# Spreading of a product-key expert layer: three chunks of the expert table rounded whole in the route, none in the first two steps, the next group rounded within the steps, and the last load moved into the experts' stage

## The chip, the cores and the metric

The kernel is one program on one NeuronCore of a Trainium2 chip. The metric is the device time of one execution in microseconds. Three runs of the kernel before gave 3746.18, 3740.43 and 3745.97 us, a median of 3745.97.

## The reference, cut to what matters

A decoder trunk of two layers over 512 tokens of 1024 channels, all in float32. Each layer is a token mixer with a layer norm and then a product-key expert layer (PEER) with a layer norm. The change lies in the expert layer:

```python
q = jnp.einsum('td,dn->tn', xt, wq).reshape(T, PEER_HEADS, 2, PEER_HALF)
s1 = jnp.einsum('thd,hkd->thk', q[:, :, 0], keys[0]); s2 = ...
v1, i1 = lax.top_k(s1, 16);  v2, i2 = lax.top_k(s2, 16)
cand = v1[..., :, None] + v2[..., None, :]           # 256 candidates a head
top_s, pos = lax.top_k(cand, 16)                     # of 128 x 128 experts
gate = jax.nn.softmax(top_s, axis=-1)
hidden = jax.nn.gelu(jnp.einsum('td,thkd->thk', xb, u_tab[eb]))
y = jnp.einsum('thk,thkd->td', gb * hidden, v_tab[eb])
```

## The kernel before, in words

The first 128 tokens ("far") take their experts' rows by gathers, with VectorE. For the other 384 tokens the kernel computes all 16384 experts densely: hidden = gelu(U x) by chunks of 128 experts, times a matrix of gates that is zero where an expert isn't chosen, times V. The table u comes in 32 groups of EC = 4 chunks, chunk = 128 experts x 1024 channels. A float32 product is made of two rounded parts: ScalarE copies a chunk of u (`ur`, raw) to its high part (`uh`), another engine subtracts to get the low part (`ul`), and TensorE multiplies three times (`matmul_split`, L97 to L99), 8 x 3 = 24 matmuls a chunk of 384 columns.

There are three stages, each an `nc.Block()` of its own with one program for each engine (sync = SP, gpsimd = POOL, tensor = PE, scalar = ACT, vector = DVE); no engine enters the next block before all have left the last one.

The route (`route_stage`, L1356 on) finds the experts of every token on VectorE, tile by tile of 128 tokens, while the other engines make the hidden values of 12 groups ahead. GpSimd makes all the low parts there (`ahead.low`, L1264). At its end come the first chunks of the next stage, by `high_for_next`, `low_for_next` (L1287) and `multiply_for_next`: chunk 0 is rounded and multiplied there, its low part by GpSimd; chunk 1 (SPLIT_AHEAD = 2) is rounded there only, its low part by VectorE after the last of its routing. That routing ends with six copy_predicated (L1599), a sum, a reciprocal and a product (L1605 to L1608); after it TensorE transposes rows, columns and gates (`turn`, L1443), and ScalarE keeps them (`keep_pairs`, L1489 to L1496).

Spreading (`spread_stage`) writes the gates, one 128 x 128 block a token, as products of one-hot matrices: 24 steps of 16 tokens. In step n VectorE makes one-hot rows (`find`, L1694, which waits until TensorE has left step n - 2, since `one_hot` and `hot_col` have two buffers) and three weighted copies (`weigh`, L1702); ScalarE makes four more rows (`one_hot_rows`, L1771 and L1774), TensorE runs four groups g of 12 matmuls (L1751), ScalarE copies each group's bank to `stage` (L1785), and SP stores two steps at a time (L1820). Beside this the stage makes the hidden values of 6 more groups, 24 chunks: a load of two chunks by SP (L1230, L897 for the next stage's), high part on ScalarE (L1259, L1282), low part on VectorE (L1264, L1287), matmuls after group g = 1, and a gelu. Before, `units_of` gives step n the second half of chunk n + 1 and the first half of chunk n + 2; `high_at` has ScalarE round chunk n + 3 in step n, `low_at` VectorE chunk n + 2. Chunks 24 and 25 are the first two of the experts' stage. Their fellows 26 and 27 are rounded after the last step, and SP issues the second half of the next group's u (`load_second(sp, 1)`) when those low parts are there. The experts' stage (`experts_stage`) begins with chunks 2 and 3 of its first group on TensorE (`hidden(0, MADE_FIRST)`).

Of the kernel before, what the change touches and what calls it, by code (L numbers as in the profile page):

```python
# [16 lines left out]
P = 128  # L17
# [3 lines left out]
KT = D_MODEL // P  # L21
# [17 lines left out]
EC = 4  # L39
# [5 lines left out]
NTB = TD // TB  # L45
AHEAD_ROUTE = 12
AHEAD_SPREAD = 6
SPLIT_AHEAD = 2
MADE_FIRST = 2
NG_AHEAD = AHEAD_ROUTE + AHEAD_SPREAD  # L50
NG_FULL = NG - NG_AHEAD
# [8 lines left out]
STEP = 16  # L60
# [54 lines left out]
def build_program(nc, a):  # L115

    with ExitStack() as whole:
# [21 lines left out]
        sem = Signals()  # L139
# [15 lines left out]
        xh = sb(whole, "xT_high", [P, KT, SEQ], F32R)  # L155
# [697 lines left out]
        for layer in range(DEPTH):  # L853
            with ExitStack() as upper:
# [76 lines left out]
                def closing_norm(ctx):  # L931
                    return Norm(ctx, "cl", carried[0], None, *carried[1:])

                experts_stage(nc, a, layer, sb, peer, bank, xh, xl, u, far, storing, sem, closing_norm, first_block, project_sems())
        kept.close()


# [422 lines left out]
def route_stage(nc, a, layer, sb, sem, bank, qT, keys, x, u, load_next, ident, iota_row, rowT, listed, gateT, gate_part,  # L1360
# [6 lines left out]
    with ExitStack() as ctx:  # L1367
# [39 lines left out]
        with nc.Block() as block:  # L1407
# [7 lines left out]
            @block.gpsimd  # L1415
            def _(pool):
                pool.sem_inc(ahead.u_low, 4)
                for chunk in range(EC * AHEAD_ROUTE):
                    ahead.low(pool, chunk // EC, chunk % EC)
                    if chunk == PER_TILE + 2:  # L1420
                        for m in range(RING):
                            far.gather(pool, m)
                ahead.low_for_next(pool, 0)

            @block.tensor
            def _(pe):
# [98 lines left out]
            def _(dve):  # L1525
                V = nc.vector
                link = make_link(dve, chain)
                for t in range(NT):
# [79 lines left out]
                    link(V.tensor_tensor(weights, gate[:], total[:].unsqueeze(2).to_broadcast([P, H, K]), ALU.mult))  # L1608
                    if t:
                        V.engine_nop().then_inc(routed, 1)  # L1610
                dve.wait_ge(ahead.next_low, 1)
                ahead.low_for_next(nc.vector, 1)


def spread_stage(nc, a, layer, sb, sem, bank, x, u, load_next, load_second, iota_row, rowT, listed, gateT, gate_part):
# [4 lines left out]
    with ExitStack() as ctx:  # L1620
# [23 lines left out]
        CHUNKS = EC * AHEAD_SPREAD  # L1644
        assert CHUNKS == STEPS

        def units_of(n):

            return [(n + 1, slice(KT // 2, KT))] * (n > 0) + [(n + 2, slice(0, KT // 2))]

        made = {c: max(c - 1, 0) for c in range(CHUNKS)}
        high_at = {c - 3: c for c in range(2, CHUNKS + 2)}
        low_at = {c - 2: c for c in range(2, CHUNKS + 2)}
        load_at, store_at = {}, {}
        for c in range(1, CHUNKS, 2):
            load_at.setdefault(max(c - 2, 0) // 2, []).append((c // EC + 1, c % EC // 2))
            store_at.setdefault(max(made[c] // 2, 1), []).append((c // EC, c % EC // 2))

        def two_ahead(step, step_for_next, eng, chunk):

# [5 lines left out]
        with nc.Block() as block:  # L1666

            @block.vector
            def _(dve):
# [39 lines left out]
                for n in range(STEPS):  # L1709
                    find(n)  # L1710
                    if n == 0:
                        split_gates(0, P, 0)
                        dve.wait_ge(gate_split, 3)
                        dve.wait_ge(found, 1)
                        weigh(n, 0, STEP // 2)
                        weigh(n, STEP // 2, STEP)
                    two_ahead(ahead.low, ahead.low_for_next, dve, low_at[n])
                    if n:
                        dve.wait_ge(gate_split, 3 if n < P // STEP else 6)
                        dve.wait_ge(found, n + 1)  # L1720
                        weigh(n, 0, STEP)
                    if n == 2:
                        split_gates(P, TD, 3)
                for c in range(MADE_FIRST, EC):
# [2 lines left out]
            @block.tensor  # L1727
            def _(pe):
                def rows_of(n, s):

                    if ROWS_BY_ACT.start <= s < ROWS_BY_ACT.stop:
                        return hot_row[:, s - ROWS_BY_ACT.start, :]
                    return one_hot[:, n % 2, STEP + (s if s < ROWS_BY_ACT.start else s - 4), :]

                def multiply(chunk, part):

                    if chunk < CHUNKS:
                        ahead.multiply(pe, chunk // EC, chunk % EC, part)
                    else:
                        ahead.multiply_for_next(pe, chunk - CHUNKS, part)  # L1740

                def body(n):
                    for g in range(4):
                        pe.wait_ge(kept, 4 * n + g + 1)
                        if g % 2 == 0:
                            pe.wait_ge(cols_hot, 2 * n + g // 2 + 1)
                        if g == 1:
                            pe.wait_ge(rows_hot_a, n + 1)
                        for s in range(4 * g, 4 * g + 4):
                            for p in range(PARTS):  # L1750
                                mm = nc.tensor.matmul(bank[g][:, s % 4 * P:(s % 4 + 1) * P], rows_of(n, s), hot_col[:, n % 2, p, s, :],  # L1751
                                                      start=p == 0, stop=p == PARTS - 1)
                        mm.then_inc(spread, 1)
                        if g == 1:
                            for chunk, part in units_of(n):
                                multiply(chunk, part)

                pe.sem_inc(spread, 4)
                pe.sem_inc(ahead.h_mm, 4)
                multiply(1, slice(0, KT))  # L1760
                for n in range(STEPS):
                    body(n)
                multiply(CHUNKS + 1, slice(KT // 2, KT))

            @block.scalar
            def _(act):
# [8 lines left out]

                def body(n):
                    b, q = n // TURNS % 2, n % TURNS
                    if n in high_at:
                        two_ahead(ahead.high, ahead.high_for_next, act, high_at[n])
                    if n == 0:  # L1780
                        ahead.gelu(act, 0, 0)
                    act.wait_ge(stored[b], 16 * (n // TURNS // 2) + 16)
                    for g in range(4):
                        act.wait_ge(spread, 4 * n + g + 5)
                        nc.scalar.activation(stage[:, b, :, q * STEP + 4 * g:q * STEP + 4 * g + 4],  # L1785
                                             bank[g][:].rearrange("p (t c) -> p c t", t=4), ACT.Copy).then_inc(kept, 1)
                        if g == 1 and n + 1 < STEPS:
                            one_hot_rows(n + 1)
                        if g == 2 and n + 1 < CHUNKS:
                            ahead.gelu(act, (n + 1) // EC, (n + 1) % EC)  # L1790

                act.sem_inc(kept, 4)
                act.sem_inc(stored[0], 16)
                act.sem_inc(stored[1], 16)
                act.sem_inc(ahead.h_act, 4)
                one_hot_rows(0)
                two_ahead(ahead.high, ahead.high_for_next, act, high_at[-1])
                for n in range(STEPS):
                    body(n)
                for c in range(MADE_FIRST, EC):  # L1800
                    ahead.high_for_next(act, c)

            @block.sync
            def _(sp):
                for r in range(2):
                    sp.sem_inc(ahead.h_out[r], 16)
                for n in range(NTB):
# [10 lines left out]
                        load_second(sp, 0)  # L1818
                    sp.wait_ge(kept, 4 * TURNS * (n + 1) + 4)
                    sp.dma_start(a["gates"][:, :, n], stage[:, b].rearrange("p (g c) t -> p g c t", c=EC)).then_inc(stored[b], 16)  # L1820
                sp.wait_ge(ahead.next_low, 4)
                load_second(sp, 1)

    return [(stored[b], 16 * (NTB // 2) + 16) for b in range(2)], [(ahead.h_out[b], 16 * AHEAD_SPREAD + 16) for b in range(2)]


def experts_stage(nc, a, layer, sb, sem, bank, xh, xl, u, far, storing, projected, closing_norm, first_block, pj):

# [5 lines left out]
    with ExitStack() as ctx:  # L1836
# [49 lines left out]
        with nc.Block() as block:  # L1886

            @block.sync
            def _(sp):
# [13 lines left out]
                def load_hidden(n, b):  # L1903
                    sp.wait_ge(w_low, EC * n)
                    sp.dma_start(hid[:, b], a["hidden"][n - NG_FULL]).then_inc(hid_in[b], 16)

                for signal, value in gates_stored + hidden_stored:
                    sp.wait_ge(signal, value)
                load_gates(0)
# [1009 lines left out]
```

## Time and profile before

| | us |
|---|---|
| median of three runs | 3745.97 |
| the profiled execution | 3748.41 |
| its span | 3746.7 |
| TensorE busy | 3679.5 |
| VectorE busy | 2775.3 |
| ScalarE busy | 1489.4 |
| GpSimd busy | 1020.9 |

The span is from the first to the last instruction, the execution's own time is somewhat longer. Busy times are sums over instructions on one engine, so the difference of TensorE's 3679.5 from the span is the time in which it stood still. A row of the timeline has the start, the duration, the engine, the line and the tiles, with "xN" where N instructions were merged; behind it in brackets the idle time before it and what ended that. In the first layer the route ends at about 938 us, spreading at about 1116 us; the second layer lies 1861 us later.

### The profile page before, as it was taken

What the parts mean: (1) busy time and instruction counts of PE and PEld (TensorE: products, weight loads), DVE (VectorE), ACT (ScalarE), POOL (GpSimd) and SP (SyncE); (2) the same over time, 40 slices, a digit from 0 to 9 for tenths busy, and PEclk for the clock granted to TensorE, in tenths of its full rate; (3) what the DMA queues carried; (4) which work ended last, traced back from release to release, by engine and by line L of the source; (5) the groups of instructions that cost most, each with busy time, mean ns of one, the idle gap of its engine ahead of it and who ended that gap; (6) DMA issues with size and microseconds to landing.
All of it is one profiled execution on the core that took longest, in us unless ns stands there. A gap on an engine that the chain in (4) does not pass through costs nothing. (4 is left out here: it accounts for less than half of the span.)

```text
span 3746.7 us, 53812 instructions
## 1 busy us (share of the span) xinstructions
PE 3679.5 (98%) x20266; PEld 3263.1 (87%) x20266; DVE 2775.3 (74%) x4663; ACT 1489.4 (40%) x2178; POOL 1020.9 (27%) x654
## 2 busy tenths in 40 slices
PE   9999999999999999999999999999999999999999
PEld 7878888999999999888888787889999999998887
DVE  5256635499988888898762665365999798888997
ACT  2254522344663333333322545233447633333332
POOL 1000000264005555554100000003640056555541
PEclk9999999999999999999999999999999999999999
DMA  4312423254689999999732225243537899999996
GB/s 157 118 61 72 172 84 141 110 187 159 217 257 375 364 360 337 358 410 387 304 130 95 75 67 172 76 148 114 202 144 234 275 371 363 356 347 349 407 389 240
DMA packets 323830, 860.20 MB, mean 230 GB/s; under 512 B 21057, under 2 KB 119361, under 8 KB 298433
## 3 DMA queue, kind: packets, MB, share of 16 engines
q1 hardware_dynamic: 249920, 589.39, 43.9%
q0 software_dynamic: 73728, 268.47, 18.7%
q8 instruction: 105, 1.72, 0.2%
q14 instruction: 77, 0.62, 0.0%
HBM read 763.41 MB, written 94.37 MB: 229 GB/s over the span
## 5 line engine op out<-in xcount | busy, mean ns | idle before, releaser
L97 PE MATMUL bank<-xT_low,u_high 128*128 128x384 f32 (+1 forms) x2144 | 731.9, 341 | 15.5 <-DVEq L2111 9.5
L99 PE MATMUL bank<-xT_high,u_low 128*128 128x384 f32 (+1 forms) x2144 | 725.3, 338 | 0.0
L98 PE MATMUL bank<-xT_high,u_high 128*128 128x384 f32 (+1 forms) x2144 | 725.1, 338 | 0.0
L97 PE MATMUL bank<-v_low,w_high 128*128 128x512 f32 x1536 | 598.5, 390 | 2.8 <-DVE v_low L2138 2.7
L98 PE MATMUL bank<-v_high,w_high 128*128 128x512 f32 x1536 | 598.1, 389 | 0.0
L99 PE MATMUL bank<-v_high,w_low 128*128 128x512 f32 x1536 | 598.1, 389 | 0.0
L1332 POOL DMA_INDIRECT far_rows<-peer_u_rows_dram,far_index x256 | 370.8, 1448 | 690.0 <-DVE far_dots L1338 637.4
L1264 POOL TENSOR_TENSOR u_low<-merged,u_high 128x1024 fp32r<-128x1024 f32 x96 | 244.3, 2559 | 1091.2 <-ACT u_high L1259 1091.2
L1332 POOL DMA_INDIRECT far_rows<-peer_v_dram,far_index x256 | 387.2, 1513 | 340.6 <-DVE x_far L1356 291.5
L2050 ACT ACTIVATE v_high<-v_raw 128x1024 fp32r<-128x1024 f32 x256 | 257.2, 1052 | 451.0 <-PE bank L99 386.9
L97 PEld LDWEIGHTS bank<-xT_low,u_high 128*128 128x128 f32 x2144 | 405.4, 189 | 22.6 <-DVEq L2111 10.1
L98 PEld LDWEIGHTS bank<-xT_high,u_high 128*128 128x128 f32 x2144 | 405.6, 189 | 4.7
L99 PEld LDWEIGHTS bank<-xT_high,u_low 128*128 128x128 f32 x2144 | 404.9, 189 | 3.7
L2138 DVE TENSOR_TENSOR v_low<-v_raw,v_high 128x1024 fp32r<-128x1024 f32 x256 | 301.5, 1219 | 125.6 <-ACT v_high L2050 125.3
L1356 DVE SCALAR_TENSOR_TENSOR x_far<-far_rows,far_dots,x_far 128x1024 f32<-128x1024 f32 x256 | 328.2, 1282 | 31.7 <-DMA far_rows<-peer_v_dram,far_index 15.4
L97 PEld LDWEIGHTS bank<-v_low,w_high 128*128 128x128 f32 x1536 | 288.4, 188 | 65.0 <-DVE v_low L2138 6.3
L99 PEld LDWEIGHTS bank<-v_high,w_low 128*128 128x128 f32 x1536 | 288.3, 188 | 60.3
L98 PEld LDWEIGHTS bank<-v_high,w_high 128*128 128x128 f32 x1536 | 288.4, 188 | 59.0
L1338 DVE CUSTOM_DVE_ANT_0 far_rows<-far_rows,x_far 128x1024 f32<-128x1024 f32 x256 | 302.4, 1218 | 19.0 <-DMA far_rows<-peer_u_rows_dram,far_index 18.9
L2044 ACT ACTIVATE w_high<-hid 128x384 fp32r<-128x384 f32 x256 | 127.7, 526 | 414.1 <-DVE hid L2129 414.1
L1259 ACT ACTIVATE u_high<-merged 128x1024 fp32r<-128x1024 f32 x140 | 147.7, 1059 | 60.4 <-DMA merged<-peer_u_dram 48.0
L1189 DVE TENSOR_TENSOR prod<-gate,bank 128x512 f32<-128x512 f32 x48 | 33.0, 688 | 163.0 <-PE bank L99 159.2
(453 smaller groups left out, 6776.9 us busy)
## 6 DMA issues: line engine op xcount, KB each, us to landing
merged<-peer_u_dram SPq DMA_DIRECT2D x128, 1024.0 KB, 6.1
v_raw<-peer_v_dram SPq DMA_DIRECT2D x128, 1024.0 KB
gates_scratch<-stage SPq DMA_DIRECT2D x24, 2048.0 KB, 8.6
G<-gates_scratch SPq DMA_DIRECT2D x64, 768.0 KB
hidden_scratch<-ahead_hid SPq DMA_DIRECT2D x72, 384.0 KB, 5.3
hid<-hidden_scratch SPq DMA_DIRECT2D x36, 768.0 KB
mg_raw<-w_merge_dram SPq DMA_DIRECT2D x28, 768.0 KB, 4.2
merged<-w_in_dram SPq DMA_DIRECT2D x20, 1024.0 KB, 6.1
```

What stands on the lines that cost most here:

```text
L97: nc.tensor.matmul(out, lh, rl, start=first, stop=False)
L98: nc.tensor.matmul(out, lh, rh, start=False, stop=False)
L99: return nc.tensor.matmul(out, ll, rh, start=False, stop=last)
L1189: V.tensor_tensor(prod[:, b, :], gate[:, b, :], bank[2 + b][:], ALU.mult).then_inc(prods, 1)
L1259: self.nc.scalar.activation(self.uh[:, c], self.ur[:, c], ACT.Copy).then_inc(self.u_high, 1)
L1264: eng.tensor_tensor(self.ul[:, c], self.ur[:, c], as_f32(self.uh[:, c]), ALU.subtract).then_inc(self.u_low, 1)
L1332: pool.indirect_dma_start(self.rows[:, m % RING, :], None, self.tables[m // PAIRS], bass.IndirectOffsetOnAxis(ap=self.index[:, slot:slot + ...
L1338: self.nc.vector.tensor_tensor_reduce(out=row, in0=row, in1=self.x[:], scale=1.0, scalar=0.0, op0=ALU.mult, op1=ALU.add, accum_out=self.do ...
L1356: self.nc.vector.scalar_tensor_tensor(out=self.x[:], in0=self.rows[:, m % RING, :], scalar=self.dots[:, m - PAIRS:m - PAIRS + 1], in1=self ...
L2044: A(wh[:, b, c, :], hid[:, b, c, :], ACT.Copy).then_inc(w_high, 1)
L2050: A(vh[:, c:c + 2, cols(r)], vr[:, c:c + 2, cols(r)], ACT.Copy).then_inc(v_high, 1)
L2138: V.tensor_tensor(vl[:, c:c + 2, cols(r)], vr[:, c:c + 2, cols(r)], as_f32(vh[:, c:c + 2, cols(r)]), ALU.subtract).then_inc(v_low, 1)
```

## The change

Four chunks are rounded in the route's end (SPLIT_AHEAD = 4), all low parts on GpSimd; TensorE multiplies chunks 1, 2 and 3 whole ahead of step 0. Steps 0 and 1 have no chunk. From step 2 on, step n multiplies chunk n + 2 whole, VectorE makes its low part in step n, ScalarE the high part of chunk n + 4 (from step 1 on). So the high and low parts of chunks 26 and 27 fall in steps 22 and 23. Loads stay in their SP blocks, stores of hidden go one block earlier, and SP issues the experts' second u load as the first thing in the experts' block.

```diff
-SPLIT_AHEAD = 2
+SPLIT_AHEAD = 4
 ...                                     # experts_stage gets first_u("ex", 1)
 ...                                     # route, gpsimd
-                ahead.low_for_next(pool, 0)
+                for c in range(SPLIT_AHEAD):
+                    ahead.low_for_next(pool, c)
 ...                                     # route, vector
-                dve.wait_ge(ahead.next_low, 1)
-                ahead.low_for_next(nc.vector, 1)
 ...                                     # spread
-        made = {c: max(c - 1, 0) for c in range(CHUNKS)}
-        high_at = {c - 3: c for c in range(2, CHUNKS + 2)}
-        low_at = {c - 2: c for c in range(2, CHUNKS + 2)}
-            load_at.setdefault(max(c - 2, 0) // 2, []).append((c // EC + 1, c % EC // 2))
-            store_at.setdefault(max(made[c] // 2, 1), []).append((c // EC, c % EC // 2))
+            block_of_c = max(c - 2, 0) // 2
+            load_at.setdefault(0 if c < EC else block_of_c, []).append((c // EC + 1, c % EC // 2))
+            store_at.setdefault(block_of_c, []).append((c // EC, c % EC // 2))
 ...                                     # spread, vector, step n
-                        dve.wait_ge(gate_split, 3)
-                        dve.wait_ge(found, 1)
-                        weigh(n, 0, STEP // 2)
-                        weigh(n, STEP // 2, STEP)
-                    two_ahead(ahead.low, ahead.low_for_next, dve, low_at[n])
-                    if n:
-                        dve.wait_ge(gate_split, 3 if n < P // STEP else 6)
-                        dve.wait_ge(found, n + 1)
-                        weigh(n, 0, STEP)
+                    if n >= 2:
+                        two_ahead(ahead.low, ahead.low_for_next, dve, n + 2)
+                    dve.wait_ge(gate_split, 3 if n < P // STEP else 6)
+                    dve.wait_ge(found, n + 1)
+                    weigh(n, 0, STEP)
 ...                                     # spread, tensor
-                        if g == 1:
-                            for chunk, part in units_of(n):
-                                multiply(chunk, part)
+                        if g == 1 and n >= 2:
+                            multiply(n + 2)
-                multiply(1, slice(0, KT))
+                for c in range(1, SPLIT_AHEAD):
+                    multiply(c)
-                multiply(CHUNKS + 1, slice(KT // 2, KT))
 ...                                     # spread, scalar, step n
-                    if n in high_at:
-                        two_ahead(ahead.high, ahead.high_for_next, act, high_at[n])
-                    if n == 0:
-                        ahead.gelu(act, 0, 0)
+                    if n:
+                        two_ahead(ahead.high, ahead.high_for_next, act, n + 4)
-                        if g == 2 and n + 1 < CHUNKS:
-                            ahead.gelu(act, (n + 1) // EC, (n + 1) % EC)
+                        if g == 2 and 2 <= n < CHUNKS - 2:
+                            ahead.gelu(act, (n + 2) // EC, (n + 2) % EC)
 ...                                     # spread, scalar, before the steps
-                two_ahead(ahead.high, ahead.high_for_next, act, high_at[-1])
+                for c in range(SPLIT_AHEAD - 1):
+                    ahead.gelu(act, 0, c)
+                two_ahead(ahead.high, ahead.high_for_next, act, 4)
+                ahead.gelu(act, 0, SPLIT_AHEAD - 1)
 ...                                     # spread, scalar, after the steps
-                for c in range(MADE_FIRST, EC):
-                    ahead.high_for_next(act, c)
 ...                                     # spread, sync, after the last gates store
-                sp.wait_ge(ahead.next_low, 4)
-                load_second(sp, 1)
 ...                                     # experts, sync, first
+                sp.wait_ge(u_low, EC)
+                load_second(sp, 1)
```

## Rows read from the trace of the kernel before

**Rows 1.** TensorE's waits: total us, times, longest; 925 to 1155, and 1870 to 2790.

```profile
PE bank L97 <- DVEq L2111: 4.8, 1, 4.8
PE bank L1751 <- DVE hot_col L1702: 3.0, 2, 2.8
PE bank L97 <- ACTq L1795: 2.0, 1, 2.0
PE bank L1443 <- DVEq L1610: 1.0, 1, 1.0
...
PE bank L2385 <- ACT prob L2547: 3.2, 2, 1.7
```

**Rows 2.** Stretches: busy us of each engine, granted clock, DMA share, GB/s.

```profile
953.90:957.20 3.30, 3.30 (x18) 3.30 (x17) 3.30 (x4) 2.69 (x7) 0.00 (x0) 0.53 0.00 0
...
1121.10:1124.50 3.40, 3.37 (x11) 3.40 (x12) 1.97 (x2) 2.62 (x4) 0.00 (x0) 0.53 1.13 347
1124.60:1147.60 23.00, 23.00 (x134) 23.00 (x133) 16.50 (x25) 10.40 (x16) 3.58 (x2) 1.00 0.96 354
...
2983.20:2988.10 4.90, 4.84 (x16) 4.87 (x16) 2.45 (x2) 2.65 (x4) 0.00 (x0) 0.51 1.06 355
...
1125.00:2799.00 1674.00, 1659.36 (x8369) 1456.45 (x8367) 1220.88 (x2185) 613.85 (x817) 504.46 (x309) 1.00 0.62 230
```

**Rows 3.** The timeline of TensorE: start, duration, line, merged count.

```profile
938.47 0.41 PE L97 MATMUL bank<-xT_low,u_high 128*128 128x384 f32 x1 [2.00 <-ACTq L1795]
...
944.29 0.84 PE L1751 MATMUL bank<-hot_col,one_hot 128*128 128x128 bf16 x12
```

**Rows 4.** The timeline of ScalarE at the route's end.

```profile
931.19 1.05 ACT L1282 ACTIVATE u_high<-merged 128x1024 fp32r<-128x1024 f32 x1
936.51 0.20 ACT L1489 ACTIVATE rowT<-bank 128x32 f32<-128x32 f32 x1 [4.27 <-PE bank L1443]
```

**Rows 5.** The timeline of VectorE at the route's end.

```profile
932.15 2.78 DVE L1599 COPY_PREDICATED found<-bit,found 128x512 f32<-128x512 uint32 x6
...
935.52 0.29 DVE L1608 TENSOR_TENSOR pgate<-pgate,total 128x128 f32<-128x128 f32 x1
938.11 0.23 DVE L1707 CAST iota_pairs<-iota_row 128x128 bf16<-128x128 f32 x1 [0.96 <-PEq L1407]
```

**Rows 6.** VectorE and GpSimd side by side in the route's first tile.

```profile
764.99 9.14 DVE L1599 COPY_PREDICATED found<-bit,found 128x512 f32<-128x512 uint32 x6
...
764.56 5.47 POOL L1264 TENSOR_TENSOR u_low<-merged,u_high 128x1024 fp32r<-128x1024 f32 x2 [3.35 <-ACT u_high L1259]
770.56 2.39 POOL L1264 TENSOR_TENSOR u_low<-merged,u_high 128x1024 fp32r<-128x1024 f32 x1 [0.52 <-ACT u_high L1259]
```

**Rows 7.** The timeline of TensorE and VectorE in steps 2 and 3.

```profile
966.95 2.19 PE L1751 MATMUL bank<-hot_col,one_hot 128*128 128x128 bf16 x36
...
961.58 2.02 DVE L1694 TENSOR_TENSOR one_hot<-iota_pairs,listed 128x3584 bf16<-128x3584 bf16 x1 [0.85 <-PE bank L1751]
966.93 1.22 DVE L1702 TENSOR_TENSOR hot_col<-one_hot,gate_low 128x2048 bf16<-128x2048 bf16 x1
```

**Rows 8.** SP's u load in a step, the stretch after it, and the gates stores' landing.

```profile
992.89 3.14 SPq L1230 DMA_DIRECT2D merged<-peer_u_dram  x1
...
1002.00:1004.00 2.00, 2.00 (x37) 2.00 (x37) 1.65 (x3) 1.12 (x3) 0.00 (x0) 1.00 0.11 38
...
gates_scratch<-stage SPq DMA_DIRECT2D x24, 2048.0 KB, 8.6
```

**Rows 9.** ScalarE, VectorE and SP at the end of spreading.

```profile
1120.96 0.49 ACT L2038 ACTIVATE hid<-bank 128x384 f32<-128x384 f32 x1 [4.20 <-PEq L1973]
...
1115.85 2.36 DVE L1287 TENSOR_TENSOR u_low<-merged,u_high 128x1024 fp32r<-128x1024 f32 x2 [8.85 <-ACT u_high L1282]
...
1114.89 0.55 SPq L1820 DMA_DIRECT2D gates_scratch<-stage  x1
1118.23 2.15 SPq L897 DMA_DIRECT2D merged<-peer_u_dram  x1
```

More of the change, by code:

```diff
@@ L932, in closing_norm @@
                     return Norm(ctx, "cl", carried[0], None, *carried[1:])
-                experts_stage(nc, a, layer, sb, peer, bank, xh, xl, u, far, storing, sem, closing_norm, first_block, project_sems())
+                experts_stage(nc, a, layer, sb, peer, bank, xh, xl, u, first_u("ex", 1), far, storing, sem, closing_norm, first_block, project_sems())
         kept.close()
@@ L1645, in spread_stage @@
         assert CHUNKS == STEPS
-        def units_of(n):
-            return [(n + 1, slice(KT // 2, KT))] * (n > 0) + [(n + 2, slice(0, KT // 2))]
-        made = {c: max(c - 1, 0) for c in range(CHUNKS)}
-        high_at = {c - 3: c for c in range(2, CHUNKS + 2)}
-        low_at = {c - 2: c for c in range(2, CHUNKS + 2)}
         load_at, store_at = {}, {}
         for c in range(1, CHUNKS, 2):
-            load_at.setdefault(max(c - 2, 0) // 2, []).append((c // EC + 1, c % EC // 2))
-            store_at.setdefault(max(made[c] // 2, 1), []).append((c // EC, c % EC // 2))
+            block_of_c = max(c - 2, 0) // 2
+            load_at.setdefault(0 if c < EC else block_of_c, []).append((c // EC + 1, c % EC // 2))
+            store_at.setdefault(block_of_c, []).append((c // EC, c % EC // 2))
         def two_ahead(step, step_for_next, eng, chunk):
@@ L1733, in rows_of, with multiply @@
                     return one_hot[:, n % 2, STEP + (s if s < ROWS_BY_ACT.start else s - 4), :]
-                def multiply(chunk, part):
+                def multiply(chunk):
                     if chunk < CHUNKS:
-                        ahead.multiply(pe, chunk // EC, chunk % EC, part)
+                        ahead.multiply(pe, chunk // EC, chunk % EC)
                     else:
-                        ahead.multiply_for_next(pe, chunk - CHUNKS, part)
+                        ahead.multiply_for_next(pe, chunk - CHUNKS)
                 def body(n):
@@ L1820, in _, with experts_stage @@
                     sp.dma_start(a["gates"][:, :, n], stage[:, b].rearrange("p (g c) t -> p g c t", c=EC)).then_inc(stored[b], 16)
-                sp.wait_ge(ahead.next_low, 4)
-                load_second(sp, 1)
     return [(stored[b], 16 * (NTB // 2) + 16) for b in range(2)], [(ahead.h_out[b], 16 * AHEAD_SPREAD + 16) for b in range(2)]
-def experts_stage(nc, a, layer, sb, sem, bank, xh, xl, u, far, storing, projected, closing_norm, first_block, pj):
+def experts_stage(nc, a, layer, sb, sem, bank, xh, xl, u, load_second, far, storing, projected, closing_norm, first_block, pj):
     V, A = nc.vector, nc.scalar.activation
```

## The prediction

> **What bounds the kernel now.** The page comes first: its busy row (in the table above) has TensorE at 3679.5 of 3746.7 us, so the time moves only where TensorE stands still, or runs at half clock. Next the list of TensorE's waits over the first layer's spreading and both its borders [rows 1]: 4.8 us at the border to the experts (L2111 is VectorE's first instruction there), 2.0 and 1.0 us at the border from the route, 3.0 us for hot_col in spreading, 2.8 of them in one wait. In the 23 us behind the experts' start it is busy without a gap [rows 2]. So this change is worth what it does at two borders and in the first three steps, twice, for the two layers.
>
> Half clock belongs to the bill. Behind the waits of 2.8 and 4.8 us the granted clock is 0.53 for 3.3 to 3.4 us, in the second layer's experts 0.51 for 4.9 us; from 1125 to 2799 us, where the longest of the waits read (1870 to 2790) is 1.7, it is 1.00 [rows 1, 2]. These are the 1.2 and the 2.4 GHz level. At full clock 134 matmuls take 23.0 us, 0.172 each and 4.1 a u chunk of 24 [rows 2]. Behind the route's border a chunk took 5.8 (944.29 - 938.47) [rows 3]: 1.7 us lost. In the slow stretches of the experts' starts 11 matmuls took 3.4 us (1.9 at full clock) and 16 took 4.9 (2.75) [rows 2]: 1.5 us lost in layer one, 2.15 in layer two.
>
> **The change, part by part.** Sums are of the profiled execution, 3746.7 us of span and 3748.4 us of its own time; the median of the runs is 3746.0, 2.4 lower. Differences carry over.
>
> (a) *End of the route: four low parts on GpSimd.* Now GpSimd makes one and VectorE the second after its routing chain. The high part of chunk 1 is made at 931.19 to 932.24 [rows 4]; new are those of chunks 2 and 3, 2 x 1.0 us, in 4.3 us in which ScalarE waits for the transposes [rows 4]: free. From 932.3 GpSimd has three low parts back to back, about 7.2 us (2.39 each [rows 6]). Exactly then VectorE runs the last six copy_predicated (932.15, 2.78 us in all) and the softmax tail up to 935.8, for which the last transposes, ScalarE's keeping of the pairs and so the next stage wait [rows 4, 5]. The nearest row shows what the two do to each other: the same six copy_predicated in tile 0 took 9.14 us instead of 2.78, with exactly three low parts of GpSimd (two from 764.56, one at 770.56) beside them [rows 6]. That is 6.4 us for three, 2.1 each. So the routing ends at 942.2, not 935.8. GpSimd itself is done at about 941.2, and VectorE stays the last. Bounds: below, VectorE is not held up, and only the barrier waits for GpSimd: 932.3 + 7.2 = 939.5, 0.4 for the barrier, against a start at 938.1 [rows 5], +1.8 us; above, each low part holds VectorE for its whole 2.4 us, +7.2. I take 6.4, the row of the same six instructions, and 0.1 for transposes at half clock: **+6.5**. The cover of the removed VectorE part (1.2 us) was the 1.2 us of ScalarE's keeping: it saves nothing.
>
> The Trainium skill, "SBUF — State Buffer", section "Who interferes with whom", says that a VectorE instruction with two SBUF inputs and a GpSimd instruction that reads SBUF exclude each other for whole instructions, and the first one keeps the pair. It speaks against this edit; by it the term would be the upper bound, 7.2, and the time below 1.6 us higher. The trace agrees with the blocking (9.14 against 2.78) and gives 2.1 for a 2.4 us instruction.
>
> (b) *First steps of spreading.* Before, counted from VectorE's start at 938.1: step 2's last matmuls end at 968.3 (966.95 + 24 of 36 matmuls) with half of chunk 4 still to do, 2.1: 32.3 us [rows 7]. After: TensorE starts 0.4 later [rows 3, 5], three chunks 3 x 4.1, half clock 1.7 [rows 3], step 0's 48 matmuls 2.7, some 0.1 between: that is at 17.2. VectorE has steps 0 and 1 ready by then (without u parts, 12 us), but its step 2 may start only when TensorE has left step 0: find, low part and three weighings, 961.58 to 968.1 [rows 7], 6.6 with the hand-overs, ready at 23.8. TensorE's step 1 lasts only 3.2 us with 0.6 for the hot rows of ScalarE, so it waits 3.4 us for hot_col, where it now waits 2.8 [rows 1]. Then step 2, 6.9 with its chunk, and the half clock behind this wait, 1.5 [rows 2]: 32.2. No gain, no loss: the wait is moved, not removed. The idle time at the border is however 7 us and more, not 3; half clock may last longer, as in the second layer's experts (2.15 against 1.5 to 1.7): **+0.6**, bounds 0 and 1.5.
>
> (c) *Inside the steps.* Per step TensorE has the same 72 matmuls (6.9 us), VectorE the same find, low and three weighings with 0.4 us to spare (6.5 of 6.9). ScalarE's high parts come one step earlier, so a load of u has about 10.4 us from its issue instead of 17. The load of 992.89 is issued over 3.1 us; the engines go quiet by 1002 to 1004 (share 0.11) [rows 8]; ScalarE wants it at about 1003.6, and has about 3 us to spare before TensorE needs its copies. It fits, by 1 us and those 3: 0. The stores of hidden go one SP block earlier, before the gates store that waits longer anyway: 0; they take away the late ahead_hid and low part of the first groups (0.3 us of TensorE): **-0.3**.
>
> (d) *End of spreading.* Now, after step 23: half a chunk; ScalarE makes high parts 2 and 3, VectorE, idle 8.85 us before, their low parts (to 1118.2), SP waits for these and issues u's second half (2.15 us, to 1120.4), and 0.6 us later ScalarE starts in the experts, TensorE at 0.75 [rows 9]. After, both parts are made in steps 22 and 23, and the load stands in the experts' block. Left after the last matmul are ScalarE's last copy and SP's gates store: the copy ends 0.65 after the last matmul, the store is issued by 1.2 (1115.44 - 1114.2), the border 0.75: 2.0 us instead of 4.75 [rows 1, 9], **-2.8**. Of 1.5 and 2.15 us of half clock behind it I count most as gone: the standstills up to 1.7 us between 1125 and 2799 us lowered it nowhere [rows 1, 2], but 2.0 is a little more, and at the route's border 2.0 with 1.0 before it did: **-1.3** a layer; bounds 0 and -2.2. The moved load now goes out about 1 us behind the gates store (8.6 us to land [rows 8]); if it needs 11 us, chunk 2 of group 1 has its parts 3 us before TensorE comes for them, 17 us into the stage. Gates and v land 2.1 us later against TensorE's start; w_low would be ready about 1 us before the output wants it. Covered, by little.
>
> Sum per layer: 6.5 + 0.6 - 0.3 - 2.8 - 1.3 = +2.7; two layers **+5.4 us**: 3746.7 to 3752.1 of span, 3753.8 of the execution's time, 3751.4 of the median.
>
> **Rivals.**
> R1, *VectorE is not held up* (not slower). If its six instructions win against GpSimd, (a) is +1.8 to 1.9: -1.9 a layer, 3742.2. For it: nothing but that the tail's instructions are shorter than those of tile 0's first ones. Against: [rows 6], where GpSimd had its turn between each two of VectorE's. It decides from the point where VectorE's tail ends before GpSimd's third low part.
> R2, *long half clock at every border*: +1.5 at the start and, with 2.0 us idle still enough to lower the clock, only -0.5 at the end: 6.5 + 1.5 - 0.3 - 2.8 - 0.5 = 4.4 a layer, 3754.8; with (a) at its upper bound 3756.4. For it: the 3 us of broken idle at the route's border.
> R3, *u arrives too late inside the steps*: each load that lands 1 us beyond the reserve stops TensorE once, 11 loads a layer: +22 us, 3773. Against: the quiet of the queues at 1002.
> R4, *the start is no loss at all and the end gives its most* (faster): (a) hidden wholly because VectorE's first steps run under it, (d) -5.0: 3739. Against: VectorE can't start before the barrier.
>
> **Numbers.** About 7 us (0.2%) is what can be told from no change. Chances: forecast 0.56, R1 0.12, R2 0.22, R3 0.05, R4 0.05. The forecast with errors of some 3 us a side lies mostly within 7.5 us of before, but its upper quarter and most of R2 are beyond: faster 0.06, same 0.56, slower 0.38. The range takes in R1's and R2's times and leaves R3 and R4 out: 3742 to 3759.
>
> **What would show it.** (a) GpSimd with three low parts back to back at the route's end and the copy_predicated beside them at 8 to 9 us in all, ScalarE's first spread instruction 6 to 7 us later; wrong if they still take 2.8. (b) One TensorE wait of 3.4 us for hot_col before step 2 and none before step 1. (c) No TensorE wait in steps 3 to 23, ScalarE's wait for merged at most 2 us a time. (d) The wait at the experts' start at 2.0 us, SP's second u load behind it, granted clock 1.00 there; wrong if it stays over 4. The forecast is wrong if (a) and (d) differ by less than 2 us or more than 6.

## The result, and the profile after

The changed kernel takes 3761.02 us (median of five runs, 3758.57 to 3762.43) against 3745.97 (3740.43 to 3746.99) for the kernel before on the same chip: a ratio of 1.0043, 95% interval 1.0028 to 1.0057. It is slower by more than can be mistaken for no change, and 2 us above the upper end of the predicted range. The profiled execution took 3762.43 us, its span is 3760.7, 14.0 more than before.

First TensorE's waits over the first layer's spreading and both its borders, 925 to 1165 us, in the kernel after (columns as in [rows 1]: total us, times, longest):

```profile
PE bank L97 <- ACT hid L2025: 5.2, 1, 5.2
PE bank L97 <- ACTq L1781: 5.1, 1, 5.1
PE bank L1740 <- DVE hot_col L1695: 3.3, 1, 3.3
PE bank L97 <- DVEq L2098: 2.2, 1, 2.2
PE bank L1740 <- ACT stage L1771: 0.9, 1, 0.9
PE bank L1740 <- ACT hot_row L1762: 0.6, 1, 0.6
PE bank L1444 <- DVEq L1611: 0.2, 1, 0.2
```

The same of the second layer, 2780 to 3030 us:

```profile
PE bank L1444 <- DVEq L1611: 6.2, 1, 6.2
PE bank L97 <- ACT hid L2025: 3.7, 1, 3.7
PE bank L1740 <- DVE hot_col L1695: 3.3, 1, 3.3
PE bank L97 <- DVEq L2098: 2.2, 1, 2.2
PE bank L97 <- ACTq L1781: 2.0, 1, 2.0
```

Against [rows 1]: the experts' border went from 4.8 to 2.2, the two waits before steps 1 and 2 became one of 3.3, the route's border has 5.3 or 8.2 instead of 3.0. All of that was in the prediction, only smaller at the route's border in layer one. Not in it was the wait for `hid` at L2025, 5.2 and 3.7 us, some 17 us into the experts' stage. There the third chunk of group 1 waits for ScalarE's gelu of that group's first chunk. The kernel before has no wait there: from 1120 to 1165 us TensorE waits only once, the 4.8 us of the border. What paces that gelu there is in the rows of ScalarE and TensorE (the kernel before, layer one):

```profile
1131.18 0.49 ACT L2038 ACTIVATE hid<-bank 128x384 f32<-128x384 f32 x1 [2.72 <-PE bank L99]
...
1132.52 2.00 ACT L2050 ACTIVATE v_high<-v_raw 128x1024 fp32r<-128x1024 f32 x2
...
1138.49 0.47 ACT L2038 ACTIVATE hid<-bank 128x384 f32<-128x384 f32 x1
...
1139.30 0.33 PE L97 MATMUL bank<-xT_low,u_high 128*128 128x384 f32 x1
```

The gelu of 1138.49 ends at 1138.96, and the first matmul that needs it (48 before the first output at 1147.62) starts at 1139.30, at TensorE's own pace. ScalarE takes v at 1132.52 without waiting for its load; what it waits for is TensorE (2.72 us, at 1131.18). So in the kernel before this chain follows TensorE, and no load.

VectorE (and under it GpSimd) at the end of the route in the kernel after, layer one, then layer two; start, duration, engine, line:

```profile
930.30 2.77 DVE L1600 COPY_PREDICATED found<-bit,found 128x512 f32<-128x512 uint32 x6
...
932.80 7.17 POOL L1287 TENSOR_TENSOR u_low<-merged,u_high 128x1024 fp32r<-128x1024 f32 x3 [8.20 <-ACT u_high L1282]
940.84 0.23 DVE L1700 CAST iota_pairs<-iota_row 128x128 bf16<-128x128 f32 x1 [5.37 <-PEq L1407]
...
2800.05 8.96 DVE L1600 COPY_PREDICATED found<-bit,found 128x512 f32<-128x512 uint32 x6
2801.18 7.47 POOL L1287 TENSOR_TENSOR u_low<-merged,u_high 128x1024 fp32r<-128x1024 f32 x3 [8.15 <-ACT u_high L1282]
```

The same six instructions took 2.77 us in layer one, because the last of them had just begun when GpSimd began its three low parts, and 8.96 in layer two, where they ran beside them.

Stretches of the kernel after (busy us of TensorE, its weight loads, VectorE, ScalarE, GpSimd, the clock, DMA share, GB/s): the start of spreading, layer one; nearly all of its spreading, with the wait of 3.3 us in it; behind the wait for `hid`; then the start of layer two's spreading, and the stretch behind its wait of 3.3 us:

```profile
940.60:947.40 6.80, 6.20 (x20) 6.23 (x21) 6.42 (x8) 2.29 (x6) 0.00 (x0) 0.52 0.77 281
957.50:1117.90 160.40, 155.57 (x1642) 151.83 (x1638) 148.12 (x115) 119.33 (x252) 0.00 (x0) 1.00 0.77 244
1142.10:1148.80 6.70, 4.93 (x16) 4.93 (x17) 6.66 (x11) 4.93 (x8) 0.23 (x1) 0.52 0.78 283
2807.80:2817.90 10.10, 5.89 (x19) 5.52 (x20) 7.21 (x12) 3.49 (x12) 0.86 (x1) 0.51 0.42 148
2838.50:2841.80 3.30, 3.30 (x17) 3.30 (x16) 3.30 (x4) 2.67 (x7) 0.00 (x0) 0.54 1.10 334
```

The time by sections of TensorE's own timeline, each from one profiled execution. A: from the route's last transposes (`pgate`) to its first matmul of spreading. B: from there to its last matmul of spreading. C: from that to its first matmul of an output (`v_low` or `v_high`). B + C holds the half chunk that the edit moved from C to B, so the two are read together. D: from C's end to the last matmul with v.

| us | A | B | C | B + C | D |
|---|---|---|---|---|---|
| before, layer 1 | 2.27 | 175.5 | 33.6 | 209.15 | 725.4 |
| after, layer 1 | 5.35 | 178.2 | 35.1 | 213.23 | 725.5 |
| before, layer 2 | 2.27 | 176.4 | 34.4 | 210.78 | 727.2 |
| after, layer 2 | 2.42 | 178.1 | 31.4 | 209.50 | 729.3 |

Layer one is 6.9 us longer at its last matmul with v, layer two 7.2 more. In layer one 2.7 come at the route's border and 4.1 in B + C. In layer two 6.4 come at the route's border (6.2 of them before the transposes), B + C is 1.3 shorter, and D 2.1 longer. D isn't touched by the edit and lies between 723.6 and 729.3 us in the traces here that meet no second door (e1 below); those 2.1 us are not explained further.

### The profile page after: what moved, and what is told of

It reads as the page before. It is cut to its first block and busy times, and to the rows that moved or that the text cites. A ratio compares the mean times of both kernels' runs of the same rounds, so it can differ in the third digit from the quotient of the medians.

```text
span 3760.7 us, 53804 instructions
## 1 busy us (share of the span) xinstructions
PE 3678.9 (98%) x20266; PEld 3262.7 (87%) x20266; DVE 2776.4 (74%) x4651; ACT 1489.6 (40%) x2178; POOL 1037.3 (28%) x660
## 5 line engine op out<-in xcount | busy, mean ns | idle before, releaser
L97 PE MATMUL bank<-xT_low,u_high 128*128 128x384 f32 (+1 forms) x2144 | 731.5, 341 | 21.9 <-ACT hid L2025 9.9
```

What stands on the lines that cost most here:

```text
L97: nc.tensor.matmul(out, lh, rl, start=first, stop=False)
```

## The experiments

Theories before the first of them: *A*, GpSimd's added low parts hold VectorE's routing tail, as the prediction had it. *D*, the experts' stage doesn't hang on when its block opens, but on the last gates store: SP waits for its landing before it loads G and v, then come v's parts, hid times G, w's parts, and the first outputs. The rivals to D: TensorE's wait for `hid` is only an over-strict bound (e1); or u's second half arrives too late since its load was moved (e2). Every run is against the kernel before on the same chip, whose median was 3744.61 for e1 to e4, 3746.16 for e5 to e8, and 3746.28 for e9 to e11.

**e1: the wait for `hid` relaxed.** TensorE's hidden(1, c) waits for three gelus beyond its own index, two more than its bank needs. The edit takes the two away for group 1.

```diff
-                            pe.wait_ge(h_act, EC * n + c + 3)
+                            pe.wait_ge(h_act, EC * n + c + (1 if isinstance(n, int) and n == 1 else 3))
```

> The kernel after, with one wait changed in the experts: chunks 2 and 3 of group 1 wait for the gelu that frees their own bank (two gelus earlier in ScalarE's order) instead of the gelu of group 1's chunk 0. Theory D (a deadline): the earlier start of the experts was given back at that wait, since ScalarE's gelu of group 1 chunk 0 hangs on the gates store, G and v, not on TensorE. Then TensorE's waits of 5.2 and 3.7 us there and the half clock behind them go, the output of group 0 starts about 25 us behind the experts' start, and the time is 9 to 13 us below the kernel after, about 3750. Rival (the same chain one door further): w_low isn't ready by then, the wait reappears before the output and the time stays at 3758 to 3761.

Measured 3760.01 us, 1.0042 (1.0028 to 1.0055): nothing gained, where some 3750 was expected. B + C fell from 213.2 to 206.6 us in layer one and from 209.5 to 205.7 in layer two, but D rose from 725.5 to 731.2 and from 729.3 to 731.4. TensorE's waits from 1165 to 1260 us, in this kernel, and VectorE's instruction just before that:

```profile
PE bank L97 <- DVE u_low L2106: 4.3, 1, 4.3
```

```profile
1206.91 1.23 DVE L1338 CUSTOM_DVE_ANT_0 far_rows<-far_rows,x_far 128x1024 f32<-128x1024 f32 x1 [2.88 <-DMA far_rows<-peer_u_rows_dram,far_index]
```

VectorE waits 2.9 us for gathered rows there and is late with a low part of u. So the `hid` wait was one door; without it TensorE runs into a second, at 1211.5 us, some 70 us on, and there gives back nearly all that it had gained.

**e2: u's second half issued ahead of the border.**

```diff
                         load_second(sp, 0)
+                        sp.wait_ge(ahead.next_low, 4)
+                        load_second(sp, 1)
...
-                sp.wait_ge(u_low, EC)
-                load_second(sp, 1)
```

> The kernel after, with SP's last u load issued in spreading's last step, ahead of the last gates store, and not in the experts. Theory D with the u load as its longest link: ScalarE no longer waits 5.0 and 4.4 us for that load, v lands some 2 us earlier since 1 MB less stands in its way, TensorE's wait before group 1 chunk 2 falls from 5.2 and 3.7 to 2 or 3 us: 3 to 6 us less than the kernel after, about 3756. Rival (v is the longest link and lands as before): ScalarE's wait only moves to v_raw, no change, 3760.

Measured 3758.96, 1.0042 (1.0028 to 1.0055). ScalarE no longer waits 4.95 us for u; it then waits for v instead. ScalarE in this kernel:

```profile
1136.83 2.01 ACT L2037 ACTIVATE v_high<-v_raw 128x1024 fp32r<-128x1024 f32 x2 [2.95 <-DMA v_raw<-peer_v_dram]
```

TensorE's wait for `hid` fell from 5.2 to 2.4 us in layer one, but rose from 3.7 to 4.2 in layer two, and B + C is 211.2 and 212.3 us. So v is the longest link, and SP issues v behind the store's landing and the load of G; that u alone came too late falls as an explanation. No run here issued v ahead of G.

**e3: low parts 1 to 3 by VectorE, after its routing, as the kernel before did with part 1.**

```diff
-                for c in range(SPLIT_AHEAD):
+                for c in range(1):
                     ahead.low_for_next(pool, c)
...
+                dve.wait_ge(ahead.next_low, 1)
+                for c in range(1, SPLIT_AHEAD):
+                    ahead.low_for_next(nc.vector, c)
```

> The kernel after, with the low parts of chunks 1, 2 and 3 made by VectorE behind its routing, GpSimd making that of chunk 0 only. Theory A (GpSimd's three low parts hold VectorE's copy_predicated, 2.1 us each): the six copy_predicated of the last tile take 2.8 us in both layers, not 9.0 in layer two, and spreading starts 3.5 us behind the routing's end: the border costs 1.5 us a layer more than in the kernel before, not 2.7 and 6.4; 5 to 6 us less than the kernel after, about 3755. Rival (the blocking is chance and the border is set by three low parts on whatever engine): no change within 2 us.

Measured 3751.21, 1.0016 (1.0006 to 1.0025): more than half of the loss gone (15.1 us became 6.6). 3755 was expected; 1.4 us of the difference is that this chip runs the kernel before faster than the first one did. VectorE in layer two of this kernel:

```profile
2795.85 2.78 DVE L1600 COPY_PREDICATED found<-bit,found 128x512 f32<-128x512 uint32 x6
...
2799.63 3.49 DVE L1287 TENSOR_TENSOR u_low<-merged,u_high 128x1024 fp32r<-128x1024 f32 x3
```

The six copy_predicated are back at 2.78 us, and the three low parts take 3.49 on VectorE where GpSimd took 7.47.

**e4: the relaxed wait in the kernel before.** The same edit as e1.

> The kernel before, with the same relaxed wait as e1_after_relaxed. Theory D: the kernel before met that deadline with 0.3 us of waiting, so nothing is gained, within 2 us of 3746. Rival (the late gelu also costs the kernel before more than its list of waits shows): 3 us or more faster.

Measured 3745.32, 1.0 (0.9991 to 1.0009). Nothing changes, since the kernel before doesn't wait there. The "0.3 us of waiting" of the expectation was read wrong: the 0.3 us for `hid` in the list of waits of before stand at 1474 us, 327 us behind the first output; at the chunks that this edit touches the list has nothing.

**e5 and e6: half of chunk 25, or all of it, put behind the last step of the kernel after.**

```diff
-                        if g == 1 and n >= 2:
+                        if g == 1 and 2 <= n < STEPS - 1:
                             multiply(n + 2)
...
                 for n in range(STEPS):
                     body(n)
+                multiply(CHUNKS + 1)
```

(e6; e5 leaves the first half of the chunk in step 23.)

> The kernel after, with the second half of chunk 25's matmuls moved from step 23 to behind the last step, as in the kernel before. Theory D (the first groups of the experts hang on the last gates store: G and v behind it, VectorE's and ScalarE's chain behind these): the store goes out 2.1 us earlier, and the experts' outputs with it, a layer: 4 us less than the kernel after, up to 7 with less half clock, about 3756. Rival S (the start of TensorE in the experts sets the pace): the half chunk stands where TensorE was idle at the border, the start is no earlier by more than 0.2 us, no change within 2 us.

> The kernel after, with the whole of chunk 25's matmuls behind the last step. Theory D: the last gates store goes out 4.2 us earlier a layer, TensorE's wait before group 1 chunk 2 shrinks from 5.2 and 3.7 us to 2 or less, 8 to 12 us less than the kernel after, about 3751. Rival S: TensorE starts the experts 2.9 us later after step 23's end than now, no gain, 3759 to 3763.

Measured 3757.34 for e5, 1.0027 (1.0016 to 1.0038), and 3753.76 for e6, 1.0019 (1.001 to 1.0028). That is 3.9 and 7.5 us less than the kernel after, each against the kernel before on its own chip. TensorE does the same work as in the kernel after; only its order differs. B + C in layer one: 213.2, then 210.4, then 209.0 us; in layer two 209.5, 209.5, 208.2. The wait for `hid` in layer one, in e5 and then in e6:

```profile
PE bank L97 <- ACT hid L2028: 4.2, 1, 4.2
```

```profile
PE bank L97 <- ACT hid L2026: 2.7, 1, 2.7
```

The step from e5 to e6 is the one that parts the two theories. From after to e5 TensorE's wait at the border falls as well, from 2.2 to 0.6 us, and that alone could make the time shorter. From e5 to e6 it stays at 0.6 in both layers; only the store goes out earlier, 4.0 us ahead of TensorE's first matmul of the experts instead of 2.1. The wait for `hid` falls from 4.2 to 2.7 and from 3.1 to 2.4, B + C by 1.4 and 1.3, the median by 3.6 us. The two ratios' intervals overlap, but only three of e6's eleven runs reach into the range of e5's seven (3754.62 to 3758.95).

**e7 and e11: the same with the kernel before.** e7 puts a whole chunk behind the last step instead of half of one, e11 one and a half.

```diff
-            return [(n + 1, slice(KT // 2, KT))] * (n > 0) + [(n + 2, slice(0, KT // 2))]
+            return [(n + 1, slice(KT // 2, KT))] * (n > 0) + [(n + 2, slice(0, KT // 2))] * (n + 1 < STEPS)
...
-                multiply(CHUNKS + 1, slice(KT // 2, KT))
+                multiply(CHUNKS + 1, slice(0, KT))
```

> The kernel before, with the first half of chunk 25's matmuls too behind the last step. Theory D: the store, the high and low parts of chunks 26 and 27 and SP's load all move 2.1 us forward and the work is done where TensorE was idle 4.8 us: 4 us less, up to 7 with less half clock, 3739 to 3742. Rival S with the load of SP as the border's last (the parts don't move forward): no change, 3746.

> The kernel before, with chunk 25 whole and the second half of chunk 24 behind the last step (one half more than e7_before_chunk_last). Theory D: the last gates store moves another 2.1 us forward a layer, TensorE's wait at the border falls from 2.7 to 0.6 us and the half clock there goes: 3 to 5 us less than e7_before_chunk_last, 3735 to 3737. Rival: the earlier experts run into VectorE's far rows, as in e8_after_best (a wait for u_low near 1205 us), and nothing is gained over e7_before_chunk_last, 3740.

Measured 3739.64 for e7, 0.9982 (0.9973 to 0.9991), and 3739.09 for e11, 0.9975 (0.9966 to 0.9985): both faster than either kernel of the case. B + C of e7 is 205.9 and 207.8, that is 3.3 and 3.0 us below before, twice about 3 of the 6.5 gained. TensorE's wait at the border is 2.7 us in both layers, for 4.8: 2.1 of the 3 us. About 1 us a layer is left. In layer two it is the clock: behind the border it is at half for 3 us, where it was for 4.9 [rows 2]. In layer one the clock stays at 1.00 at the route's border, where [rows 3] had half, and that was not followed further. e11 has 204.3 and 207.9, but in layer one D grew to 731.9 (725.4 before): the second door of e1 again, now `DVE u_low` with 3.0 us. One chunk takes most of what is there: 0.5 us between the medians can't be told from nothing.

**e9: the reverse, no matmul behind the last step of the kernel before.** This move of half a chunk had no term of its own in the prediction.

```diff
+            if n == STEPS - 1:
+                return [(n + 1, slice(KT // 2, KT)), (n + 2, slice(0, KT))]
...
-                multiply(CHUNKS + 1, slice(KT // 2, KT))
```

> The kernel before, with the second half of chunk 25's matmuls inside step 23, ahead of the last gates store, as the change has it, and nothing else of the change. Theory D: the last store, and the experts' outputs behind it, come 2.1 us later a layer: 4 us slower than the kernel before, 3750. Rival (this part of the change is neutral, the loss is in the ends and starts of other engines): 3746, within 2 us.

Measured 3750.35, 1.0009 (1.0 to 1.0018), 4.1 us more than before: slower, by about what the interval can still part from nothing. B + C rose by 2.6 and 1.8 us. TensorE's wait at the experts' border in this kernel:

```profile
PE bank L97 <- DVEq L2112: 6.9, 1, 6.9
```

The half chunk is 2.1 us of cover at this border, and 4.8 [rows 1] became 6.9 in both layers: 4.2 us for the two, about the whole of the loss. That theory D forecast the right time here and for e7 is luck: in both kernels ScalarE takes v without a wait and TensorE doesn't wait for `hid`. What they measure is the cover at the border, not the chain behind the store.

**The hour of the last gates store.** SP's rows in layer one and ScalarE's gelu on which the third chunk of group 1 waits; first the kernel after, then e7 (the kernel before has its store in [rows 9] and its gelu in the section on the result):

```profile
1120.24 0.55 SPq L1807 DMA_DIRECT2D gates_scratch<-stage  x1
...
1128.72 0.33 SPq L1886 DMA_DIRECT2D G<-gates_scratch  x1
1129.10 1.03 SPq L1882 DMA_DIRECT2D v_raw<-peer_v_dram  x2
...
1137.55 2.00 ACT L2037 ACTIVATE v_high<-v_raw 128x1024 fp32r<-128x1024 f32 x2 [3.51 <-DMA v_raw<-peer_v_dram]
1141.57 1.87 ACT L2031 ACTIVATE w_high<-hid 128x384 fp32r<-128x384 f32 x4 [2.01 <-DVE hid L2116]
1143.34 0.47 ACT L2025 ACTIVATE hid<-bank 128x384 f32<-128x384 f32 x1
```

```profile
1109.09 0.55 SPq L1820 DMA_DIRECT2D gates_scratch<-stage  x1
1132.81 0.47 ACT L2038 ACTIVATE hid<-bank 128x384 f32<-128x384 f32 x1
```

The same two rows in other kernels, with the waits beside them, layer one and layer two:

| us | border wait | ScalarE's wait for v | from store to gelu | TensorE's wait for it |
|---|---|---|---|---|
| before | 4.8, 4.8 | none | 23.6, 24.3 | none |
| e9 | 6.9, 6.9 | none | 24.2, 24.0 | none |
| e7 | 2.7, 2.7 | none | 23.7, 23.6 | none |
| e11 | 1.9, 2.5 | 1.1, none | 24.5, 25.7 | 0.6, none |
| after | 2.2, 2.2 | 3.5, 2.5 | 23.1, 21.6 | 5.2, 3.7 |
| e2 | 2.2, 2.2 | 3.0, 4.7 | 21.9, 22.1 | 2.4, 4.2 |
| e3 | 2.2, 2.2 | 2.9, 2.2 | 22.4, 21.8 | 3.0, 3.9 |
| e5 | 0.6, 0.6 | 3.1, 2.4 | 22.7, 21.6 | 4.2, 3.1 |
| e6 | 0.6, 0.6 | 3.0, 2.1 | 23.0, 22.7 | 2.7, 2.4 |

Theory D holds for the kernel after and its variants: ScalarE waits for v in both layers of every one, and the gelu comes 21.6 to 23.1 us behind the store, though the border wait varies. (In e8, below, it is 25.3 and 26.1: there the store itself took 12.5 and 13.2 us to land, for 8.4 in the kernel after.) It doesn't hold for the kernel before and its variants. Only the first layer of e11 waits for v; in the others the first matmul that needs the gelu starts 0.3 us behind the gelu's end every time, because the gelu follows TensorE's own chunks. So the edit took TensorE from its own pace into a deadline that the kernel before had met.

**e10: part (a) at its smallest, one low part, in the kernel before.**

```diff
-                ahead.low_for_next(pool, 0)
+                for c in range(SPLIT_AHEAD):
+                    ahead.low_for_next(pool, c)
...
-                dve.wait_ge(ahead.next_low, 1)
-                ahead.low_for_next(nc.vector, 1)
```

> The kernel before, with the low part of chunk 1 made by GpSimd and not by VectorE behind its routing, and nothing else of the change. Theory A: this one low part holds one of the last six copy_predicated for 2.1 us (they take 4.9 us, not 2.8), and the last transposes come 2.1 us later a layer: 3 to 4 us slower, about 3750. Rival: VectorE's tail wins and GpSimd runs behind it; the border is unchanged, 3746.

Measured 3751.4, 1.001 (1.0001 to 1.0019). VectorE at the end of the route in both layers of this kernel, with GpSimd's low part in the first:

```profile
929.65 4.98 DVE L1600 COPY_PREDICATED found<-bit,found 128x512 f32<-128x512 uint32 x6
932.08 2.39 POOL L1287 TENSOR_TENSOR u_low<-merged,u_high 128x1024 fp32r<-128x1024 f32 x1 [8.46 <-ACT u_high L1282]
...
2793.60 4.84 DVE L1600 COPY_PREDICATED found<-bit,found 128x512 f32<-128x512 uint32 x6
```

One low part holds the six for 2.2 and 2.1 us, so three for 6.2 to 6.4: a price per instruction, as [rows 6] had it. (This profiled execution, 3745.76 us, is one of the fastest of the kernel's eleven, 3745.48 to 3754.06.)

**e8: e1, e2, e3 and e6 together in the kernel after.**

> The kernel after with four things together: low parts 1 to 3 by VectorE (e3_after_dve_lows), the whole of chunk 25 behind the last step (e6_after_chunk_last), the relaxed wait (e1_after_relaxed) and the early u load (e2_after_u_early). Theories A and D: the 7 to 9 us of e3_after_dve_lows and the 8 to 12 of e6_after_chunk_last add up, 3741 to 3745, the level of the kernel before or a little below. Rival: they don't add, since the earlier experts run into VectorE's far rows (TensorE waits 4 us for u_low near 1208 us), 3748.

Measured 3751.59, 1.0017 (1.0008 to 1.0026): no better than e3 alone, where 3741 to 3745 was expected. B + C is 203.1 and 202.9 us, the shortest of all, and D 732.1 and 732.0. TensorE's waits for `u_low` in the two layers:

```profile
PE bank L97 <- DVE u_low L2110: 4.4, 1, 4.4
...
PE bank L97 <- DVE u_low L2110: 5.7, 1, 5.7
```

The gains don't add, since all of them move TensorE toward the same second door, and that one hardly moves: it opens 269.5 and 271.4 us behind the start of spreading here, 269.3 and 271.3 in e11, 273.0 and 272.0 in e1. What sets its hour was not tested.

## Why the prediction was wrong, point by point

(a) *End of the route, +6.5 a layer.* Mechanism shown (e3, e10), size right in layer two (+6.4). In layer one it was +2.7. The prediction let GpSimd begin 0.15 us behind the first of the six (932.3 against 932.15), as the profiled kernel before had it in layer one. That was the odd case: of the thirteen traces ScalarE's high part, on which GpSimd waits, is ready 2.3 to 2.4 us behind the first of the six in ten, and 0.1, 0.2 and 0.7 behind in three; in layer two it is 1.05 to 1.44. At 2.4 us VectorE has only its last copy_predicated left. In the kernel after, e5 and e6 it had just begun and the six took 2.77; in e1 and e2 GpSimd came 0.1 us sooner, held that last one, and the six took 4.98 and 4.97. A term that depends on such a meeting should have been given as two cases, and not as one. Besides, VectorE came to the six 1.9 us earlier in this execution (930.30 against 932.15 of [rows 5]) though the code ahead of them is the same; counted from there the border is 4.6 us longer, not 2.7. The Trainium skill, "SBUF — State Buffer", section "Who interferes with whom", says that a VectorE instruction with two inputs in SBUF contends with a GpSimd instruction that reads SBUF, and that their shared ports are held for a whole instruction. That agrees with e10: one copy_predicated was held and took 2.2 and 2.1 us more, beside a GpSimd instruction of 2.39.

(b) *First steps, +0.6.* Right: one wait of 3.3 us for hot_col (3.4 predicted), none before step 1 but the 0.6 for hot rows. The half clock behind it came in layer two alone. B, less the half chunk of 2.1 us, is +0.5 in layer one and -0.4 in layer two.

(c) *Inside the steps, -0.3.* Right: no wait for u in steps 3 to 23, in either layer, one of 0.9 us for a bank's copy. R3 falls.

(d) *End of spreading, -4.1 a layer: the step that failed.* The border itself came as forecast, 2.2 us for 2.0, and in both layers at full clock. But the prediction closed the account there, with "Gates and v land 2.1 us later against TensorE's start; w_low would be ready about 1 us before the output wants it. Covered, by little." What it measured, with the half chunk counted, is +3.6 us in layer one (B + C +4.1, less 0.5) and -0.9 in layer two (-1.3 and +0.4).

Two things were wrong. First the size of the shift: from the issue of the last gates store to TensorE's first matmul of the experts 6.2 us passed before (1121.13 - 1114.89) and 1.5 after (1121.78 - 1120.24). So gates and v come 4.7 us later against TensorE's start, 2.1 for the half chunk and 2.6 for the shorter border; and as TensorE has no half clock behind the border, 6.2 us later in layer one and 6.9 in layer two by the third chunk of group 1. Second the link: only w_low was looked at. The tighter one is the gelu that ScalarE makes in order behind v's and w's high parts, on which the third chunk of group 1 waits. By the table above that gelu came 23.6 and 24.3 us behind the store in the kernel before, and 0.3 us before TensorE wanted it; with v as its pace it comes 23.1 and 21.6 behind. So the kernel before had 0.8 and 3.1 us in hand (estimates: 23.6 - 23.1 + 0.3, 24.3 - 21.6 + 0.3, unrounded), the edit took 6.2 and 6.9, and 5.4 and 3.8 were to come back as a wait; 5.2 and 3.7 came. In layer one the standstill brought its own half clock, 6.7 us at 0.52. The step from e5 to e6 shows the chain by itself; relaxing the wait (e1) didn't give the time back, because the second door stands behind it.

The sum: +2.7 a layer was forecast, and 6.8 and 7.2 came. Layer one is (a) 3.8 us lower and (d) 7.7 higher; layer two is (a) as forecast, (d) 3.2 higher, (b) and (c) 0.7 lower and 2.1 in D, which stay open. R4 fell with the route's border; its 3739 also doesn't follow from its terms, which give -4.7 a layer and 3736.6. R2 (long half clock) came true in half: in layer two the route's border had 10.1 us at 0.51, but the end's border had none, so it isn't what carried the time beyond 3759. R1's mechanism held in layer one alone.

## What to carry to other kernels

A shorter wait at the start of a stage is worth only what its next deadline leaves: follow the chain that the border doesn't start, here from a store of the stage before. How much time is in hand there can't be read from a list of waits, which had nothing at this place; it is read from the hour at which a result is ready and the hour at which it is asked for, and from whether the chain follows a load or the engine itself. A wait in such a list has a place too: look where it stands before an argument is built on it. Work that nobody waits for belongs where the engine would stand still, behind the last store that somebody waits for: 2 us of matmuls moved into that border made the kernel before 6.5 us faster, and out of it 4.1 slower. And an instruction given to an idle engine is priced by what it does to the busy one beside it, which is 2.1 us for each low part of GpSimd here, when they meet.

## What the runs showed of the hardware

The same standstill lowered TensorE's clock in one place and not in another. In the kernel after, the wait of 3.3 us before step 2 is followed by a granted clock of 1.00 in layer one and by 3.3 us at 0.54 in layer two; behind the border wait of 2.2 us it stays at 1.00 in both, and behind the 3.7 us for `hid` in layer two as well (first row). In the first layer of e1, with the same border wait of 2.2, it doesn't stay (second row, a mean over a stretch that holds about 3 us at half clock):

```profile
3014.00:3017.40 3.40, 3.40 (x20) 3.40 (x21) 3.35 (x5) 3.15 (x4) 0.00 (x0) 1.00 0.90 314
...
1118.70:1145.00 26.30, 26.30 (x144) 26.30 (x144) 14.64 (x19) 12.79 (x19) 0.00 (x0) 0.94 1.01 365
```

Half clock lasted 10.1 us where 6.2 and 2.0 us of idle time followed each other, 6.7 behind the single 5.2, and 3.3 behind 3.3. Whether a standstill of 2 to 4 us brings it could not be told from anything in these rows; it is an uncertainty of about 1.6 us for each of them, not a term. And VectorE's six copy_predicated took 2.78, 4.98 and 8.96 us with none, one and three low parts of GpSimd beside them.
